# Adding up squares on GpSimd instead of on TensorE, in the two norms behind a residual

## The reference, cut to what matters

```python
def rms_norm(x, g, eps=NORM_EPS):
    x32 = x.astype(jnp.float32)
    y = x32 * lax.rsqrt(jnp.mean(x32 * x32, axis=-1, keepdims=True) + eps)
    return (y * g.astype(jnp.float32)).astype(x.dtype)
...
        h = h + rms_norm(mix @ w_out[l], ln_attn_post[l])
        hn = rms_norm(h, ln_ffn_pre[l])
        u = causal_dwconv(hn @ w_up[l], conv_w[l], conv_b[l])
...
        h = h + rms_norm(f, ln_ffn_post[l])
    return h
...
        h = rmsnorm(x, norm_mix_g[l])
        x = x + gated_branch_mixer(h, w_in[l], ...)
```

## Time and profile before

| | us |
|---|---|
| median of three runs (lowest, highest) | 1659.87 (1659.46, 1661.07) |
| span of the profiled execution, first to last instruction | 1655.9 |
| left over between span and median | 4.0 |
| TensorE busy | 1530.4 (92%) |
| VectorE busy | 1093.5 (66%) |
| ScalarE busy | 705.5 (43%) |
| GpSimd busy | 57.3 (3%) |

### The profile page before, as it was taken

How to read it: one execution, slowest core, us unless ns; L and a number is a source line. 1 busy time by engine, 2 the same in 40 slices (tenths; PEclk the granted TensorE clock), 3 DMA queues, 4 the chain that set the end, 5 groups by cost and what they waited for, 6 DMA issues and landing times.

```text
span 1655.9 us, 26753 instructions
## 1 busy us (share of the span) xinstructions
PE 1530.4 (92%) x11012; PEld 1284.9 (78%) x11012; DVE 1093.5 (66%) x1661; ACT 705.5 (43%) x1057; POOL 57.3 (3%) x52
## 2 busy tenths in 40 slices
PE   5999988998999999999999999999999888788892
PEld 4889777876878888888878787787898667788892
DVE  5831776686499637637689997455765445677775
ACT  5422444443344333323454222234344346367773
POOL 0000000000000000000000000000000000232121
PEclk9999999999999999999999999999999999999996
DMA  6220000002412222222312222232243103688995
GB/s 249 102 94 9 2 3 3 2 3 78 170 59 102 81 98 102 102 102 85 119 56 98 102 98 81 102 115 102 77 153 134 70 26 112 212 273 324 333 343 209
DMA packets 37832, 189.74 MB, mean 115 GB/s; under 512 B 4305, under 2 KB 4433, under 8 KB 24401
## 3 DMA queue, kind: packets, MB, share of 16 engines
q1 hardware_dynamic: 30672, 167.08, 28.1%
q0 software_dynamic: 4864, 16.78, 2.8%
q10 hardware_dynamic: 2176, 4.19, 0.8%
HBM read 175.46 MB, written 12.58 MB: 114 GB/s over the span
## 4 chain that ended last, share of the span: by engine, by line
PE 70%; DVE 17%; DMA 4%; ACT 4%; issue 3%; POOL 0%; SPq 0%; POOLq 0%; DVEq 0%; ACTq 0%
PE acc L474 18%; PE acc L476 18%; PE acc L475 18%; DMA raw<-wstream 3%; DVE CA L2439 2%; PE acc L725 2%; PE mb L725 1%; DVE wl L1958 1%; DVE wl L1970 1%; ACT wh L1254 1%; PE acc L1032 1%; PE mb L556 1%; DVE sqa L1887 1%; PE mb L610 1%; ACT wh L1267 1%
## 5 line engine op out<-in xcount | busy, mean ns | idle before, releaser
L474 PE MATMUL acc<-XH,wh 128*128 128x512 f32 x1008 | 396.3, 393 | 2.2 <-DVE wl L1970 1.3
L476 PE MATMUL acc<-XH,wl 128*128 128x512 f32 x1008 | 392.4, 389 | 0.0
L475 PE MATMUL acc<-XL,wh 128*128 128x512 f32 x1008 | 392.2, 389 | 0.0
L1267 ACT ACTIVATE wh<-raw 128x2048 fp32r<-128x2048 f32 x99 | 189.3, 1914 | 242.0 <-DMA raw<-wstream 242.0
L1970 DVE TENSOR_TENSOR wl<-raw,wh 128x2048 fp32r<-128x2048 f32 x99 | 226.1, 2287 | 67.2 <-ACT wh L1267 64.0
L474 PEld LDWEIGHTS acc<-XH,wh 128*128 128x128 f32 x1008 | 189.2, 188 | 44.6 <-issue 3.2
L475 PEld LDWEIGHTS acc<-XL,wh 128*128 128x128 f32 x1008 | 189.2, 188 | 40.8 <-issue 1.9
L476 PEld LDWEIGHTS acc<-XH,wl 128*128 128x128 f32 x1008 | 189.2, 188 | 39.6
L1288 ACT ACTIVATE ev<-acc 128x512 f32<-128x512 f32 x146 | 85.5, 597 | 216.7 <-PE acc L476 187.2
L1958 DVE TENSOR_TENSOR wl<-raw,wh 128x1024 fp32r<-128x1024 f32 x96 | 116.5, 1223 | 39.7 <-ACT wh L1254 39.3
L1254 ACT ACTIVATE wh<-raw 128x1024 fp32r<-128x1024 f32 x96 | 100.7, 1059 | 32.1 <-DMA raw<-wstream 31.7
(11 more groups left out here) (533 smaller groups left out, 2768.2 us busy)
## 6 DMA issues: line engine op xcount, KB each, us to landing
raw<-wstream SPq DMA_DIRECT2D x99, 1024.0 KB, 4.8
raw<-wstream SPq DMA_DIRECT2D x96, 512.0 KB, 6.1
YG<-YT ACTq DMA_DIRECT2D x8, 512.0 KB, 6.0
XT<-xT SPq DMA_DIRECT2D x2, 1024.0 KB, 9.7
XT<-xT SPq DMA_DIRECT2D x1, 2048.0 KB, 7.8
XD<-HN SPq DMA_DIRECT2D x4, 512.0 KB, 2.6
out<-XTK SPq DMA_DIRECT2D x4, 512.0 KB, 2.6
cst<-consts SPq DMA_DIRECT2D x1, 1230.0 KB, 18.5
```

The costliest lines, as they stand in the source:

```text
L474: mm(out_, a[0], b[0], start=start, stop=False)
L475: mm(out_, a[0], b[1], start=False, stop=False)
L476: return mm(out_, a[1], b[0], start=False, stop=stop)
L1267: actv(wh[:, n % RING].rearrange("p a b c -> p (a b c)"), raw[:, n % RING, :], ACT.Copy).then_inc(hi_done, 1)
```

## The change

For norms 2 and 4 the squares are no longer multiplied with ones on TensorE one by one. GpSimd waits for each square, copies the first into `sqa` and adds the other seven to it. TensorE multiplies `sqa` with ones once, and does so in the second raw block after its k = 1 (norm 0 keeps its place at the end of the first block). ScalarE's root waits for that one product.

```diff
-SUMMED = (2, 4)
+ON_POOL = (2, 4)
...
         def _(pool):
+            for r in ON_POOL:
+                for k in range(KT):
+                    q = KT * r + k
+                    pool.wait_ge(sq_ready, q + 1)
+                    if k == 0:
+                        nc.gpsimd.tensor_copy(sqa[:, :], sq[:, 0, :]).then_inc(sq_used, 1)
+                    else:
+                        pool.wait_ge(sq_used, q)
+                        nc.gpsimd.tensor_tensor(sqa[:, :], sqa[:, :], sq[:, k % 2, :], ALU.add).then_inc(sq_used, 1)
+
             pool.wait_ge(s["stored"], 16 * TT)
...
-                        if b == 0 and r in SUMMED:
-                            pe.wait_ge(sq_ready, KT * r + k + 1)
-                            mm(mb[:, 0, :], ones, sq[:, k % 2, :], start=(k == 0),
-                               stop=(k == KT - 1)).then_inc(sq_used, 1)
-                        elif b == 0 and k == KT - 1:
+                        if (b, k) == ((1, 1) if r in ON_POOL else (0, KT - 1)):
                             pe.wait_ge(sq_used, KT * (r + 1))
                             mm(mb[:, 0, :], ones, sqa[:, :], start=True, stop=True).then_inc(st_sum, 1)
...
                 if r in WIDE:
-                    if r in SUMMED:
-                        act.wait_ge(sq_used, KT * (r + 1))
-                    else:
-                        act.wait_ge(st_sum, OTHERS[r])
+                    act.wait_ge(st_sum, OTHERS[r])
```

More of the change, by code:

```diff
@@ L59 @@
 OPERANDS = {0: 0, 2: 8, 4: 16, 6: 24, 7: 32}
-SUMMED = (2, 4)
+ON_POOL = (2, 4)
 WIDE = (0, 2, 4)
-OTHERS = {r: sum(x not in SUMMED for x in range(r + 1)) for r in range(9)}
+OTHERS = {r: r + 1 for r in range(9)}
 NARROW = {r: sum(x not in WIDE for x in range(r + 1)) for r in range(9)}
```

## The result

The changed kernel takes 1675.28 us (median of 5 runs, 1669.38 to 1681.25), the kernel before in the same round of runs 1661.07 (1659.46 to 1664.11). The ratio is 1.0074, with an interval of 1.0048 to 1.0101. A second set of 6 runs later gave 1676.17 and 1.0103 [1.0066, 1.0140]. (The ratio is estimated from all runs; the medians alone give 1.0086 the first time.) So by the medians the change costs 14 to 16 us, by the ratios 12 to 17, with TensorE relieved of 28 matmuls. The forecast was 1672.4, in a range from just above 1660 to 1681.

A forecast was written before the change was run, and what follows sets the result against it. The prediction took the root's start at norms 2 and 4 as the bound, not TensorE's busy time. Its terms, 5.5 + 5.5 + 1.5 = 12.5 us, moved 1659.9 to 1672.4 us, range from just above 1660 to 1681.

The forecast's parts named there:

- The chain from the root: Behind ScalarE's root at norms 2 and 4: rigid, so any delay of the root passes in full to TensorE's restart.
- Root to restart: From ScalarE's root until TensorE resumes after its wait: stays 22.7 us at norm 2 and 88.4 us at norm 4.
- The root decides: At norms 2 and 4 one number counts: how much earlier or later ScalarE's root starts.
- The root with a free GpSimd: Without disturbance by GpSimd, the 12 matmuls ahead of the sum put the root 0.6 us later at each norm.
- GpSimd's add: One add of a 128x512 tile on GpSimd, taken as 1.25 us, with 3.35 us as the slow end.
- The shared reads: In VectorE's loop, GpSimd's adds conflict over SBUF reads: root 4.4 to 6.5 us later, 5.5 taken at each norm.
- The code load: Loading GpSimd's add code behind its first copy, taken as 6.1 us, delays norm 2 only, by 1.5 us.
- The clock: TensorE's granted clock may fall on the 12 matmuls ahead of the sum, adding up to 2.8 us; no separate chance.
- first step: What bounds the kernel: TensorE time saved in the two raw blocks, 12.2 us over both norms, turns into idle time.
- No conflict: Rival: GpSimd and VectorE read SBUF undisturbed; +2.7 us, 1662.6, or +6 us with a long load; chance 0.20.
- The slow adder: Rival: GpSimd's add, towards 3.35 us, sets the loop's pace; +18 us, 1678; chance 0.13 together with a long load.
- The other side: Rival: the chain from the root is not rigid and TensorE's time counts; 4.2 us gained, 1655.7; chance 0.05.

The follow-up runs named there:

- e5: Changed kernel with the same adds done by VectorE, two tiles behind, instead of GpSimd: 1671.89 us, ratio 1.0077.
- e8: The changed kernel measured once more, nothing altered: 1676.17 us, ratio 1.0103.
- e1: Changed kernel with each GpSimd add on one column of 512, the other columns left out of the sum: 1668.78 us, ratio 1.0046.
- e2: Changed kernel with each GpSimd add replaced by a memset that writes all columns and reads none: 1664.28 us, ratio 1.0020.
- e3: Changed kernel with the product with ones right behind the first raw block, 12 matmuls sooner: 1671.29 us, ratio 1.0060.
- e4: Kernel before, with squares and ones of norms 2 and 4 rounded to fp32r, each product one matmul instead of two: 1656.87 us, ratio 0.9984.
- e9: Changed kernel with 13 small filler matmuls ahead of TensorE's fourth block in ffn and tenth in mix, where it sat idle: 1667.49 us, ratio 1.0062.
- e11: Kernel before, with one-pass fp32r products at norms 2 and 4, each placed ahead of its k's six matmuls: 1655.23 us, ratio 0.9976.

## Why the prediction was right, and where its sum was not

**The chain from the root: right.** Root to restart is 22.67 us before and after, in e5 and e8, and 22.68 in e1 and e2. TensorE's saved time all became idle time. "The root decides" is too short, though: the reciprocal decides, and it needs the root's end and the end of VectorE's splits. In e3 and e4 root to restart was 24.29 and 23.59 us. At norm 4 it is 88.38 us before and after, as forecast.

**The root with a free GpSimd, +0.6 us: right**, measured in e1 and e2 (22.49 and 22.47 against 21.90).

**GpSimd's add, 1.25 us: a little low.** It takes 1.34 us where it is not held up (at 483.11) and 1.48 to 1.83 in the loop. The other end, 3.35 us, was far off.

**The shared reads: right in kind, 5.5 us taken, 4.6 measured.** The range worked out was a mean period of 2.68 to 3.04 us; the trace shows 2.72, near the better end, though not by the pattern behind it. (Its upper end comes out as 2.99 from its own rows, the mean of 2.05 + 1.25 and 2.68; that changes little.) The adds don't evade the two-operand operations; the engine that starts second is stretched. The Trainium skill (SBUF — State Buffer, Who interferes with whom) says this of reads from SBUF by both engines, and that a GpSimd instruction which only writes does not contend. The traces agree on both: 3.39 us for a split of 2.28 beside the add, 2.28 beside the memset. The one that starts second loses a little less than the other's whole rest: XRL 1.03 us of 1.22.

**The code load, +1.5 us at norm 2: wrong.** The copy ends, and 0.23 us later the first add starts, at norm 2; at norm 4 the gap is 0.22 us, and both roots are equally late (26.50 and 26.49). The term is 0. The 6 us of the Trainium skill (GPSIMD Engine Reference, Instruction dispatch) at a first call appear between no two rows here. The load instruction stands in the trace at 466.6 us, behind the copy, and takes 3 ns; when code was loaded, if it was, the trace does not tell.

**The clock: the term that was missing.** The prediction named a fall of the clock, but on the 12 matmuls ahead of the sum, and that one did not come. The first block's stretch:

```profile
463.00:484.00 21.00, 13.59 (x63) 9.54 (x62) 20.59 (x25) 10.91 (x17) 11.98 (x8) 1.00 0.00 0
```

TensorE was busy for 13.59 of 21 us there, at a granted clock of 1.00, and the 12 matmuls from 485.33 to 488.05 came 0.23 us apart. The prediction's own first step had said that TensorE's saved time turns into idle time, and took idle time to be free. It isn't: 3.6 us of it were followed by matmuls at 1.2 GHz, at both restarts. It also expected TensorE's busy time to fall by about 12 us; between the two profiles it rose by 8.3, with slower matmuls in them.

**The sum.** Forecast 12.5 = 5.5 + 5.5 + 1.5 us. Measured 4.6 + 4.6 = 9.2 us by the roots (e9: 8.5 in the time), and 14.2 and 15.5 us in all, so 5 to 6 us are not the roots'. In the changed kernel's trace some 3 us of them are the two falls at the restarts and 1.5 us the longer wait at norm 3; falls at other places, which differ from execution to execution, make up the rest. The median came within 3 us of the forecast because 3.3 us too much stood in the terms for the reads and the code load, and 5 to 6 us were missing. That the total is so close is luck; that it is slower, and by the roots first, is not.

**The rivals.** No conflict falls by 1.77 against 0.74 us. The slow adder falls by 1.34 us, and by GpSimd's waits of 1.9 us. The other side, TensorE's time counts, falls by the unchanged 22.67 us.

**Open.** What makes the clock fall at 179 and 227 us, ahead of anything changed, in some executions; they are part of a spread between executions: 12 and 19 us in the changed kernel's two sets, 15 us over the 78 runs of the kernel before beside the experiments. Why the clock did not fall behind 3.60 us of idle time in e2, and 2.52 us in e3. Why weights land later at norm 3 where the idle time was long.

## What to carry to other kernels

Before work is moved off the busiest engine, find what ends last at that place: here it was the reciprocal, which waits for the root and for VectorE's own queue, and moving eight products ahead of their blocks was worth more than removing seven. Work given to GpSimd that reads wide SBUF tiles costs VectorE about as much as doing it (0.67 against 0.60 us for an add), if VectorE reads two such tiles at the time. Time freed on TensorE just ahead of a wait may be paid for behind it by a lower clock; look at the granted clock behind the wait, not only at the idle time.

## What was unexpected of the hardware

- Idle times of 3.55 to 3.63 us were followed by 3.4 to 6.8 us at 1.2 GHz in ten of eleven cases, and by none in e2 at norm 4. Idle times of 1.87, 2.10, 2.30, 2.52 and 2.93 us were followed by a fall (e4, e11, e3; granted 0.66 from 501 to 505 in e11), one of 2.52 us in e3 was not (1.00 from 505 to 517). So the length of the idle time alone doesn't say it. None of 1.34 us or less was followed by one. Fillers that left 0.7 us idle kept the clock at 1.00.
- The stretching isn't always the whole of the other's rest: XRL, started 0.6 us into an add, took 1.03 us more; L1940, started 1.02 us into one, 0.32 more. The add is stretched too, from 1.34 to 1.82 and 1.49 us, for it starts within 0.01 us of L1940 or while XRL still runs.
- GpSimd's add on 128x1 takes 0.23 us where it is free and 0.74 us where it starts with a VectorE operation of two SBUF operands; on 128x512 it takes 1.34 us, its copy 1.18 us (always begun beside an XRL), its memset 0.53 us.
- The 128x512 product with ones takes two matmuls in fp32, listed together with 1.02 us, and one in fp32r, 0.39 us.
